# Second slabs' low parts on GpSimd or inside the norm, the last squares of a norm summed by TensorE, and the root ahead of the split

## The chip, the cores and the metric
The kernel runs on one core of a Trainium2 chip. The metric is device time in microseconds (us) of one execution. The profile is of one execution, taken by the hardware profiler; in it PE is TensorE's matmuls, PEld its weight loads, DVE is VectorE, ACT ScalarE, POOL GpSimd, SP the queue of SyncE that issues most DMAs. L12 is line 12 of the kernel before.

## What is computed
Two transformer blocks and a hybrid block with a mixture of experts, for one sequence of 512 tokens and 1024 channels, all in float32. What bears on the change is that every layer begins with an RMS norm of the residual stream h, modulated by a scale and a shift, and then multiplies by a large weight matrix:

```python
def rms_norm(x, g):
    xf = x.astype(jnp.float32)
    y = xf * lax.rsqrt(jnp.mean(xf * xf, axis=-1, keepdims=True) + EPS)
    return (y * g.astype(jnp.float32)).astype(x.dtype)

sh, sc, gt = _ada(mod, 0)
h = h + 0.5 * gt * swiglu(modulate(rms_norm(h, norm_g[l, 0]), sh, sc), ffn_w_in[l, 0], ffn_w_out[l, 0])
u = modulate(rms_norm(h, norm_g[l, 1]), sh, sc)
y = dilated_mixer(u, ...)          # layer 0;  nsa_mixer(u, ...) in layer 1
h = h + gt * y
h = h + 0.5 * gt * swiglu(modulate(rms_norm(h, norm_g[l, 2]), sh, sc), ffn_w_in[l, 1], ffn_w_out[l, 1])
# behind layer 0: shared_kv of the normed h; behind layer 1: hybrid_mixer, then peer_ffn
```

## The kernel before
**Data.** h lies in SBUF as eight tiles of 128 channels x 512 tokens (KT = 8). The normed and modulated x is kept as a high part xh (rounded to the matmul's format) and a low part xl (the rest). All weights come from one array of 331 slabs, 128 x 2048 float32 (1 MB) each, in the order in which they are used. A slab goes through three steps, in two alternating slots: load_slab (SP, into raw, waits on raw_free), split_hi (ScalarE rounds it into whi, waits on the load and on slab_used, TensorE's count of slabs it is done with) and split_lo (VectorE writes wlo = raw - whi and counts raw_free up). Three matmuls a product (hi x hi, hi x lo, lo x hi) follow when slab_ready (raw_free) says so.

**Stages.** They run one after another, each a block of its own with a program for every engine, and a barrier of all engines between two blocks: init, ffn00, the dilated attention (qkv projection, attention, twice, then the projection awo), ffn01, shared_kv (wkv), ffn10, the nsa attention (projection wq, attention, projection bwo), ffn11, the mixer (win, branches, wout), and peer. f is the number of a stage's first slab. The first slab's parts for a stage are made in the stage before it. Before the change so are the second slab's in all but qkv and ffn00. Where a norm's tail ends the stage, the high part is made by ScalarE ahead of the root (L495 in the ffn stages, L1039 in stage_out_projection) and the low part by VectorE behind the reciprocal (L540, L1083); shared_kv makes ffn10's at its end, which stays as it is.

**The tail of a norm.** As TensorE finishes the output tiles of an ffn's second matrix or of a projection, VectorE adds each into h (L533, L1071 or L1073), ScalarE squares it (norm_square, L299) into a ring of two tiles, and VectorE adds the squares one by one into `total` (norm_add, L308). TensorE's norm_total, when its last product is out, runs seven products that nobody reads (L314), sums `total` over its 128 channels by four matmuls against ones (L323; the profile counts two passes each), runs three more unread products, and spreads the result: ScalarE takes the root of it (norm_std, L346), VectorE the reciprocal (norm_rinv, L359), and TensorE's norm_spread (L366) copies it to all 128 partitions of a PSUM bank. Three unread products end the block.

**The head.** The next block begins with norm_start on TensorE (five unread products), and norm_low on VectorE with norm_high on ScalarE: for each of the eight tiles VectorE writes the scaled tile, h x gain x root, from SBUF and PSUM into a ring of two (L392), ScalarE adds the shift and rounds it into xh (L374), and VectorE writes xl = scaled + shift - xh (L398), whose two tiles lie in SBUF. One scaled tile is made ahead. TensorE takes the first slab tile by tile behind them (L413 to L417; L427 to L431 in qkv and wq, where its first slab has tiles 0 to 3 and the second slab tiles 4 to 7). `between` is a hook that norm_high calls behind tile 2 and norm_low behind tile 4; ffn00 makes its second slab there. In qkv of the first half the second slab is split after all eight tiles.

## Time and profile before

| | us, if nothing else is said |
|---|---|
| device time, median of 3 (lowest, highest) | 4014.19 (4013.3, 4015.83) |
| span of the profiled execution, first to last instruction | 4013.5 |
| TensorE busy | 3869.2 (96%) |
| VectorE busy | 2602.8 (65%) |
| ScalarE busy | 1598.1 (40%) |
| GpSimd busy | 556.3 (14%) |
| mean granted TensorE clock (1 is 2.4 GHz, 0.5 is 1.2 GHz) | 0.985 |

The profile gives no other time of that execution than its span. The norm boundaries are at these times of the span (the reciprocal, L359): 408.7 between ffn00 and qkv, 1009.4 between awo and ffn01, 1379.7 between ffn01 and wkv, 1811.7 between ffn10 and wq, 2112.6 between bwo and ffn11, 2481.5 between ffn11 and win, 2719.7 between wout and peer. A row of a timeline gives the start, the duration, the engine, the line, the operation with what it writes and reads, how many were merged (x3), and in brackets how long the engine was idle before it and what ended that. Starts of matmuls follow each other by 0.227 us at the full clock while each lasts 0.39, since they overlap.

### The profile page before, as it was taken

The numbers are of one execution on the slowest core, as the hardware profiler recorded it, in microseconds if no ns is written. First come the engines' busy times: TensorE is split into PE (matmuls) and PEld (weight loads), VectorE is DVE, ScalarE is ACT, GpSimd is POOL, SyncE is SP. The second block draws the span as 40 slices with busy tenths as digits, with TensorE's granted clock in tenths as the row PEclk, the third lists the DMA queues.
The fourth block names the chain that finished last, engine by engine and source line by source line (L and its number), as shares of the span: only waits on it lengthen the run. The fifth ranks groups of instructions, "written<-read, shape, count | busy, mean of one in ns | idle before, by whom it ended". The sixth has DMA issues, their size and how long they took to land. (4 is left out here: it accounts for less than half of the span.)

```text
span 4013.5 us, 54684 instructions
## 1 busy us (share of the span) xinstructions
PE 3869.2 (96%) x19575; PEld 3241.7 (81%) x19575; DVE 2602.8 (65%) x4763; ACT 1598.1 (40%) x2237; POOL 556.3 (14%) x565
## 2 busy tenths in 40 slices
PE   7999999999999989998999999999999999999998
PEld 6888786887888878886668887668889999988886
DVE  6642776766663466427854324768998888687887
ACT  3222335335322232225863222543346666533333
POOL 1100000000110011000000000000015555233332
PEclk9999999999999989998999999989999999999999
DMA  7632321322662256323012222113349999899997
GB/s 285 228 130 94 135 98 45 112 89 79 221 224 95 109 178 226 131 89 93 1 64 95 94 100 89 64 42 117 118 170 342 350 351 348 308 353 353 352 357 271
DMA packets 140839, 702.11 MB, mean 175 GB/s; under 512 B 18791, under 2 KB 20166, under 8 KB 95182
## 3 DMA queue, kind: packets, MB, share of 16 engines
q1 hardware_dynamic: 66734, 424.29, 29.2%
q0 software_dynamic: 73952, 275.81, 19.1%
q8 instruction: 92, 1.51, 0.2%
q14 instruction: 61, 0.50, 0.0%
HBM read 637.06 MB, written 59.80 MB: 174 GB/s over the span
## 5 line engine op out<-in xcount | busy, mean ns | idle before, releaser
L112 DVE TENSOR_TENSOR w_lo<-raw,w_hi 128x2048 fp32r<-128x2048 f32 x331 | 758.5, 2292 | 700.1 <-ACT w_hi L104 697.9
L124 PE MATMUL ps<-x_hi,w_hi 128*128 128x512 f32 (+1 forms) x2768 | 1032.3, 373 | 20.4 <-DVE w_lo L112 16.0
L125 PE MATMUL ps<-x_lo,w_hi 128*128 128x512 f32 (+1 forms) x2768 | 1022.7, 369 | 0.0
L126 PE MATMUL ps<-x_hi,w_lo 128*128 128x512 f32 (+1 forms) x2768 | 1022.2, 369 | 0.0
L104 ACT ACTIVATE w_hi<-raw 128x2048 fp32r<-128x2048 f32 x331 | 632.5, 1911 | 650.0 <-PE ps L126 421.4
L124 PEld LDWEIGHTS ps<-x_hi,w_hi 128*128 128x128 f32 x2768 | 521.0, 188 | 94.6 <-issue 17.4
L125 PEld LDWEIGHTS ps<-x_lo,w_hi 128*128 128x128 f32 x2768 | 521.1, 188 | 68.3
L126 PEld LDWEIGHTS ps<-x_hi,w_lo 128*128 128x128 f32 x2768 | 520.7, 188 | 67.7
L2483 POOL DMA_INDIRECT ph_rows<-in_peer_u,ph_names x88 | 156.8, 1782 | 1201.5 <-DVE ph_names L2855 981.5
L2566 PE MATMUL ps<-w_hi,px_gh 128*128 128x512 f32 x768 | 299.0, 389 | 2.0 <-issue 1.6
L2566 PE MATMUL ps<-w_lo,px_gh 128*128 128x512 f32 x768 | 298.8, 389 | 0.0
L2566 PE MATMUL ps<-w_hi,px_gl 128*128 128x512 f32 x768 | 298.8, 389 | 0.0
L480 ACT ACTIVATE silu<-ps 128x512 f32<-128x512 f32 x88 | 52.6, 598 | 560.1 <-PE ps L126 559.0
L124 PE MATMUL ps<-hid_hi,w_hi 128*128 (+1 forms) x704 | 273.9, 389 | 0.0
L126 PE MATMUL ps<-hid_hi,w_lo 128*128 (+1 forms) x704 | 273.9, 389 | 0.0
L125 PE MATMUL ps<-hid_lo,w_hi 128*128 (+1 forms) x704 | 273.9, 389 | 0.0
L133 PE MATMUL ps<-w_hi,x_hi 128*128 128x512 f32 (+1 forms) x672 | 257.2, 383 | 7.1 <-DVE w_lo L112 4.8
L134 PE MATMUL ps<-w_lo,x_hi 128*128 128x512 f32 (+1 forms) x672 | 255.7, 380 | 0.0
L135 PE MATMUL ps<-w_hi,x_lo 128*128 128x512 f32 (+1 forms) x672 | 255.6, 380 | 0.0
L510 DVE TENSOR_TENSOR silu<-silu,ps 128x512 f32<-128x512 f32 x88 | 60.4, 687 | 285.9 <-ACT silu L480 285.9
L184 DVE SCALAR_TENSOR_TENSOR ada_ring<-ada_ring,ps 128x1024 f32<-128x1024 f32 x160 | 187.7, 1215 | 19.6 <-DMA ada_ring<-in_w_ada 13.5
L2566 PEld LDWEIGHTS ps<-w_hi,px_gh 128*128 128x128 f32 x768 | 144.2, 188 | 32.6 <-issue 1.9
(432 smaller groups left out, 5661.6 us busy)
## 6 DMA issues: line engine op xcount, KB each, us to landing
raw<-in_slabs SPq DMA_DIRECT2D x331, 1024.0 KB, 4.9
ada_ring<-in_w_ada POOLq DMA_DIRECT2D x160, 512.0 KB, 5.6
act_dram<-px_act SPq DMA_DIRECT2D x64, 384.0 KB, 6.6
gate_dram<-ps_g SPq DMA_DIRECT2D x12, 2048.0 KB, 11.6
px_g<-gate_dram POOLq DMA_DIRECT2D x32, 768.0 KB, 8.1
px_ai<-act_dram POOLq DMA_DIRECT2D x64, 384.0 KB, 6.5
h_dram<-h SPq DMA_DIRECT2D x2, 2048.0 KB
h<-h_dram SPq DMA_DIRECT2D x2, 2048.0 KB, 8.2
```

Source lines behind the costliest of these rows:

```text
L104: k.nc.scalar.activation(k.whi[:, c % 2, :], k.raw[:, c % 2, :], ACT.Copy).then_inc(k.hi_in, 1)
L112: nc.vector.tensor_tensor(k.wlo[:, c % 2, :], k.raw[:, c % 2, :], k.whi[:, c % 2, :].bitcast(F32), ALU.subtract).then_inc(k.raw_free, 1)
L124: mm(out, hi, rhs_hi, start=start, stop=False)
L125: mm(out, hi, rhs_lo, start=False, stop=False)
L126: return mm(out, lo, rhs_hi, start=False, stop=stop)
L133: mm(out, x_hi, hi, start=start, stop=False)
L134: mm(out, x_hi, lo, start=False, stop=False)
L135: return mm(out, x_lo, hi, start=False, stop=stop)
L184: ve.scalar_tensor_tensor(slot, slot, 1.0, self.c, ALU.mult, ALU.mult, accum_out=k.mod[:, bass.ds(16 * i + m + 8 * self.base, 1)]).then_in ...
L510: nc.vector.tensor_tensor(sil[:, c % 2, :], sil[:, c % 2, :], bank(k, 2 + c % 2), ALU.mult).then_inc(prod_ready, 1)
L2483: gp.indirect_dma_start(row_of(n), None, d["peer_u" if n < P else "peer_v"], bass.IndirectOffsetOnAxis(names[:, n % P:n % P + 1], 0)).then ...
L2566: last = nc.tensor.matmul(bank(k, 2 * r + dh), x, w[:, slot, at:at + T], start=first and half == 0 and n == 0, stop=final and half == 1 an ...
```

## The change
It has four parts.

1. **Low parts on GpSimd.** ffn01, ffn11, shared_kv, the mixer's first stage and peer get a GpSimd program (or a first step in it) that makes the second slab's low part, second_lo. It is gone from VectorE at the end of the stage before. VectorE waits for it behind norm_low (second_lo_done).
2. **Low parts inside the norm.** In wq the second slab's low part is made by VectorE behind tile 4 of norm_low; in qkv of the first half so too, and its high part by ScalarE behind tile 2 of norm_high. For that the first of three rounds in qkv's programs for ScalarE and VectorE is written out ahead of the loop.
3. **Sums by TensorE.** VectorE adds the squares of six of the eight tiles; those of the last two are summed over channels by TensorE directly from the ring, before and after `total`. The three unread products behind norm_spread go.
4. **The root ahead of the split.** ScalarE takes the root (norm_std) before it makes the high part of the second slab.

```diff
+def second_lo(k, gp, f):
+    gp.wait_ge(k.hi_in, f + 2)
+    k.nc.gpsimd.tensor_tensor(k.wlo[:, (f + 1) % 2, :], k.raw[:, (f + 1) % 2, :], k.whi[:, (f + 1) % 2, :].bitcast(F32),
+                              ALU.subtract).then_inc(k.raw_free, 1)
+
+
+def second_lo_done(k, ve, f):
+    ve.wait_ge(k.raw_free, f + 4)
...
+BY_ADDS = KT - 3
+
+
+def norm_total(k, pe, total, ring, rb=SUM_BANK):
     x, w = k.xh[:, 0, 0:P], k.xl[:, 0, :]
     pe.wait_ge(k.n["h"], KT * k.norms + 2)
     unread_products(k, 0, x, w, 7)
-    pe.wait_ge(k.n["summed"], KT * k.norms + KT - 1)
-    for b in range(NB):
-        last = k.nc.tensor.matmul(bank(k, SUM_BANK, 1, b), total[:, b * P:(b + 1) * P], k.ones[:, 0:1],
-                                  start=b == 0, stop=b == NB - 1)
-    last.then_inc(k.n["summed"], 1)
+
+    def sums(squares, first=False, final=False):
+        for b in range(NB):
+            last = k.nc.tensor.matmul(bank(k, SUM_BANK, 1, b), squares[:, b * P:(b + 1) * P], k.ones[:, 0:1],
+                                      start=first and b == 0, stop=final and b == NB - 1)
+        return last
+    pe.wait_ge(k.n["sq"], KT * k.norms + KT - 1)
+    sums(ring[:, (KT - 2) % 2, :], first=True)
+    pe.wait_ge(k.n["summed"], KT * k.norms + BY_ADDS)
+    sums(total)
+    pe.wait_ge(k.n["sq"], KT * k.norms + KT)
+    sums(ring[:, (KT - 1) % 2, :], final=True).then_inc(k.n["summed"], KT - BY_ADDS)
     unread_products(k, 0, x, w, 3)
     norm_spread(k, pe, rb, k.norms + 1)
-    unread_products(k, 0, x, w, 3)
...
+        by_gpsimd = name in ("ffn01", "ffn11")
...
             if ada:
                 ada.load_c(gp, d)
+            if by_gpsimd:
+                second_lo(k, gp, f)
...
+            norm_std(k, act)
             if f > 0:
                 split_hi(k, 0, f + n_in + n_out + 1)
-            norm_std(k, act)
...
-                if n > 1:
+                if 1 < n <= BY_ADDS + 1:
                     norm_add(k, ve, n - 1, sil, total)
-            norm_add(k, ve, KT - 1, sil, total)
             norm_rinv(k, ve)
-            if f > 0:
-                split_lo(k, 0, f + n_in + n_out + 1)
...
+            if hf == 0:
+                norm_high(k, act, rot, norm[1], lambda: split_hi(k, 0, f + 1))
+                group(0, True)
+                with act.Fori(0, 2) as g:
+                    group(g + 1)
...
+            if hf == 0:
+                norm_low(k, ve, rot, norm[0], norm[1], SUM_BANK, permuted=True, between=lambda: split_lo(k, 0, f + 1))
...
             for m in range(KT - 2, KT):
                 norm_square(k, act, m, m, ring, total)
+            norm_std(k, act)
             split_hi(k, 0, f + 5)
-            norm_std(k, act)
...
-            norm_add(k, ve, KT - 2, ring, total)
-            norm_add(k, ve, KT - 1, ring, total)
             norm_rinv(k, ve)
-            split_lo(k, 0, f + 5)
...
-            norm_low(k, ve, q[:, 0], norm[0], norm[1], SUM_BANK)
+            norm_low(k, ve, q[:, 0], norm[0], norm[1], SUM_BANK, between=lambda: split_lo(k, 0, f + 1))
...
             norm_low(k, ve, ct, mod[0], mod[1], SUM_BANK)
+            second_lo_done(k, ve, f)
```

TensorE between bwo's last product and ffn11's head, before (L314 unread products, L323 the sum against ones, L366 the spread; L979 and L542 are the end of one block and the start of the next):

```order
5923 L314 MATMUL ps<-x_lo,x_hi 128x512 [waits norm_h]
5924 L314 MATMUL ps<-x_lo,x_hi 128x512 x6
5925 L323 MATMUL ps<-ones,norm_ring 128x1 [waits norm_summed]
5926 L323 MATMUL ps<-ones,norm_ring 128x1 x3
5927 L314 MATMUL ps<-x_lo,x_hi 128x512 x3
5928 L366 MATMUL ps<-ident,norm_r 128x128 [waits norm_r4]
5929 L366 MATMUL ps<-ident,norm_r 128x128 x3
5930 L314 MATMUL ps<-x_lo,x_hi 128x512 x3
5931 L979 UNCONDITIONAL_BRANCH
5932 L542 UNCONDITIONAL_BRANCH [waits barrier_Pool_Activation_PE_DVE_SP_release]
```

The same place of the same engine after (line numbers are the changed kernel's: L324 unread products, L337 sums, L385 the spread):

```order
5935 L324 MATMUL ps<-x_lo,x_hi 128x512 [waits norm_h]
5936 L324 MATMUL ps<-x_lo,x_hi 128x512 x6
5937 L337 MATMUL ps<-ones,norm_ring 128x1 [waits norm_sq]
5938 L337 MATMUL ps<-ones,norm_ring 128x1 x3
5939 L337 MATMUL ps<-ones,norm_ring 128x1 [waits norm_summed]
5940 L337 MATMUL ps<-ones,norm_ring 128x1 x3
5941 L337 MATMUL ps<-ones,norm_ring 128x1 [waits norm_sq]
5942 L337 MATMUL ps<-ones,norm_ring 128x1 x3
5943 L324 MATMUL ps<-x_lo,x_hi 128x512 x3
5944 L385 MATMUL ps<-ident,norm_r 128x128 [waits norm_r4]
5945 L385 MATMUL ps<-ident,norm_r 128x128 x3
5946 L1019 UNCONDITIONAL_BRANCH
```

One sum has become three, each with a wait of its own, and nothing stands between the spread and the end of the block. The other six tails of this form read alike.

ScalarE at the same place, before (L104 is split_hi, L299 the squares, L346 the root):

```order
894 L104 ACTIVATE w_hi<-raw 128x2048 [waits slab_used,raw_in0]
895 L299 ACTIVATE norm_ring<-h 128x512 [waits norm_summed,norm_h] x4
896 L104 ACTIVATE w_hi<-raw 128x2048 [waits slab_used,raw_in1]
897 L346 ACTIVATE norm_r<-ps,eps 128x4 [waits norm_summed]
898 L979 UNCONDITIONAL_BRANCH
```

ScalarE there after (L309 the squares, L365 the root):

```order
919 L104 ACTIVATE w_hi<-raw 128x2048 [waits slab_used,raw_in0]
920 L309 ACTIVATE norm_ring<-h 128x512 [waits norm_summed,norm_h] x4
921 L365 ACTIVATE norm_r<-ps,eps 128x4 [waits norm_summed]
922 L104 ACTIVATE w_hi<-raw 128x2048 [waits slab_used,raw_in1]
923 L1019 UNCONDITIONAL_BRANCH
```

The second slab's high part is now the last instruction of ScalarE's block.

GpSimd from the end of the nsa attention to the first gather of peer, after (L118 is second_lo; L71 clears semaphores between blocks):

```order
222 L71 ISA x5
223 L488 UNCONDITIONAL_BRANCH
224 L118 TENSOR_TENSOR w_lo<-raw,w_hi 128x2048 [waits hi_in]
225 L462 UNCONDITIONAL_BRANCH
226 L71 ISA [waits barrier_Pool_Activation_PE_DVE_SP_gather]
227 L71 ISA x4
228 L1970 UNCONDITIONAL_BRANCH
229 L118 TENSOR_TENSOR w_lo<-raw,w_hi 128x2048 [waits hi_in]
230 L1965 UNCONDITIONAL_BRANCH
```

Before, GpSimd had no instruction in these blocks but the clearing of semaphores; now a 128x2048 subtraction is the first of ffn11's and of the mixer's.

## Rows read from the trace of the kernel before

**Rows 1.** Page, first part: busy us, share of the span, instructions of each engine.
```profile
PE 3869.2 (96%) x19575; PEld 3241.7 (81%) x19575; DVE 2602.8 (65%) x4763; ACT 1598.1 (40%) x2237; POOL 556.3 (14%) x565
```

**Rows 2.** Timeline (start, us, engine, line, operation), TensorE, tail of bwo.
```profile
2108.79 1.75 PE L314 MATMUL ps<-x_lo,x_hi 128*128 128x512 f32 x7
2111.19 1.05 PE L323 MATMUL ps<-ones,norm_ring 128*128 128x1 f32 x8 [0.65 <-DVE norm_ring L308]
2112.10 0.94 PE L314 MATMUL ps<-x_lo,x_hi 128*128 128x512 f32 x3
2112.88 1.08 PE L366 MATMUL ps<-ident,norm_r 128*128 128x128 f32 x8
2113.72 0.94 PE L314 MATMUL ps<-x_lo,x_hi 128*128 128x512 f32 x3
2115.32 1.40 PE L314 MATMUL ps<-w_hi 128*128 128x512 f32 x5 [0.66 <-PEq L979]
```

**Rows 3.** Timeline, ScalarE and VectorE, the same tail of bwo.
```profile
2110.31 1.89 ACT L104 ACTIVATE w_hi<-raw 128x2048 fp32r<-128x2048 f32 x1
2112.28 0.26 ACT L346 ACTIVATE norm_r<-ps,eps 128x4 f32<-128x4 f32 x1
...
2112.67 2.26 DVE L112 TENSOR_TENSOR w_lo<-raw,w_hi 128x2048 fp32r<-128x2048 f32 x1
```

**Rows 4.** Timeline, TensorE and VectorE, tail of ffn01.
```profile
1374.90 1.75 PE L314 MATMUL ps<-x_lo,x_hi 128*128 128x512 f32 x7
...
1379.24 0.94 PE L314 MATMUL ps<-x_lo,x_hi 128*128 128x512 f32 x3
...
1379.81 2.26 DVE L112 TENSOR_TENSOR w_lo<-raw,w_hi 128x2048 fp32r<-128x2048 f32 x1
```

**Rows 5.** Timeline, TensorE, tail of ffn10, at the half clock.
```profile
1812.61 1.91 PE L366 MATMUL ps<-ident,norm_r 128*128 128x128 f32 x8
1814.17 1.19 PE L314 MATMUL ps<-x_lo,x_hi 128*128 128x512 f32 x3
```

**Rows 6.** Timeline of qkv's head, and one stretch: its us, busy of five engines, clock.
```profile
422.18 0.73 DVE L398 SCALAR_TENSOR_TENSOR x_lo<-dp_rot,mod,x_hi 128x512 fp32r<-128x512 f32 x1
...
423.99 0.74 DVE L398 SCALAR_TENSOR_TENSOR x_lo<-dp_rot,mod,x_hi 128x512 fp32r<-128x512 f32 x1
...
430.82 0.80 PE L133 MATMUL ps<-w_hi,x_hi 128*128 128x512 f32 x1 [4.78 <-DVE w_lo L112]
...
435.95 0.39 PE L133 MATMUL ps<-w_hi,x_hi 128*128 128x512 f32 x1
...
430.80:434.00 3.20, 3.18 (x8) 2.51 (x9) 2.90 (x4) 0.00 (x0) 0.00 (x0) 0.50 0.58 195
```

**Rows 7.** Timeline, GpSimd and VectorE in nsa; one line of the source view (ns min/median/max).
```profile
1986.73 1.04 POOL L1557 CAST nsa_q<-nsa_qT 64x1024 fp32r<-64x1024 f32 x1 [5.16 <-PE ps L1570]
...
1986.70 0.69 DVE L1730 CUSTOM_DVE_ANT_0 na_sm<-ps,nsa_causal 128x512 f32<-128x512 f32 x1
...
1987.44 0.35 DVE L1736 SCALAR_TENSOR_TENSOR na_ng<-na_mx,nsa_rs 128x4 f32<-128x4 f32 x1
...
1901.62 0.17 DVE L1736 SCALAR_TENSOR_TENSOR na_ng<-na_mx,nsa_rs 128x4 f32<-128x4 f32 x1
...
L1730 DVE CUSTOM_DVE_ANT_0 na_sm<-ps,nsa_causal x128: 280/486/692, 1881.6 to 2049.3; 128x128 f32<-128x128 f32 x32, 128x256 f32<-128x256 f32 x32, 128x384 f32<-128x384 f32 x32, 128x512 f32<-128x512 f32 x32
```

**Rows 8.** Timeline, VectorE and GpSimd, head of wq; GpSimd's first in ffn01.
```profile
1815.79 1.41 DVE L392 SCALAR_TENSOR_TENSOR nq_q<-h,gain,ps 128x512 f32<-128x512 f32 x2 [1.71 <-PEq L443]
1817.32 0.75 DVE L398 SCALAR_TENSOR_TENSOR x_lo<-nq_q,mod,x_hi 128x512 fp32r<-128x512 f32 x1
...
1818.77 0.75 DVE L398 SCALAR_TENSOR_TENSOR x_lo<-nq_q,mod,x_hi 128x512 fp32r<-128x512 f32 x1
...
1816.33 0.14 POOL L1342 MEMSET nq_kcp<- 64x64 f32 x1 [185.66 <-POOLq L443]
...
1014.30 0.57 POOL L163 DMA_DIRECT2D ada_ring<-in_c_rows  x1 [240.69 <-issue]
```

More of the change, by code:

```diff
@@ L465, in _ @@
             two_step(sp, n_in + n_out, lambda i, c: load_slab(k, sp, i, c), f + 2)
-        if ada:
-            @blk.gpsimd
-            def _(gp):
+        by_gpsimd = name in ("ffn01", "ffn11")
+        @blk.gpsimd
+        def _(gp):
+            if ada:
                 ada.load_c(gp, d)
+            if by_gpsimd:
+                second_lo(k, gp, f)
+            if ada:
                 with gp.Fori(0, 3) as i:
@@ L709, in _, with group @@
             act.sem_inc(s["trc"], 4)
-            if hf == 0:
-                norm_high(k, act, rot, norm[1])
-            with act.Fori(0, 3) as g:
+            def group(g, first=False):
                 for c in range(3):
-                    split_hi(k, 3 * g, f + 2 * c + 1)
+                    if not (first and c == 0):
+                        split_hi(k, 3 * g, f + 2 * c + 1)
                     if c > 0:
@@ L726, in _ @@
                         nc.scalar.activation(ss[:], ss[:], ACT.Sqrt).then_inc(s["std"], 1)
+            if hf == 0:
[3 more added lines that the diff above has]
+                    group(g + 1)
+            else:
+                with act.Fori(0, 3) as g:
+                    group(g)
         @blk.vector
@@ L731, in _, with group @@
             ve.sem_inc(s["freed"], 4)
-            if hf == 0:
-                norm_low(k, ve, rot, norm[0], norm[1], SUM_BANK, permuted=True)
-            ve.wait_ge(s["const"], 32)
-            with ve.Fori(0, 3) as g:
+            def group(g, first=False):
                 for c in range(3):
-                    split_lo(k, 3 * g, f + 2 * c + 1)
+                    if not (first and c == 0):
+                        split_lo(k, 3 * g, f + 2 * c + 1)
                     if c == 2:
@@ L778, in _ @@
                             ve.wait_ge(s["rot"], n)
+            if hf == 0:
+                norm_low(k, ve, rot, norm[0], norm[1], SUM_BANK, permuted=True, between=lambda: split_lo(k, 0, f + 1))
+            ve.wait_ge(s["const"], 32)
+            if hf == 0:
+                group(0, True)
+                with ve.Fori(0, 2) as g:
+                    group(g + 1)
+            else:
+                with ve.Fori(0, 3) as g:
+                    group(g)
     k.heads += hf == 0
@@ L1129, in stage_shared_kv, with _ @@
         k2 = k.ps[0:NC, 7 * T:7 * T + 2 * HD].rearrange("p (h d) -> p h d", h=2)
+        @blk.gpsimd
+        def _(gp):
+            second_lo(k, gp, f)
         @blk.sync
@@ L1230, in _ @@
             norm_low(k, ve, ct, mod[0], mod[1], SUM_BANK)
+            second_lo_done(k, ve, f)
             ve.wait_ge(s["const"], 80)
@@ L1926, in stage_mixer_in, with _ @@
         blk = ctx.enter_context(nc.Block(no_gpsimd_drain=True))
+        @blk.gpsimd
+        def _(gp):
+            second_lo(k, gp, f)
         @blk.sync
@@ L1980, in _ @@
             norm_low(k, ve, sig, norm[0], norm[1], SUM_BANK)
+            second_lo_done(k, ve, f)
             split_lo(k, 0, f + 2)
@@ L2485, in gather @@
                     asked[0] = n + 1
+            second_lo(k, gp, f)
             gp.wait_ge(s["names"], HEADS)
@@ L2913, in _ @@
             norm_low(k, ve, norm_ring, norm[0], norm[1], 5)
+            second_lo_done(k, ve, f)
             ve.wait_ge(s["const"], 48)
```

6 lines of the change are left out of this document (3 added, 3 removed).

## The prediction
> **What bounds the kernel now.** First the page's busy shares: TensorE works for 96% of the span [rows 1], so time can only be won or lost where it waits or runs slow. What the change touches is seven norm boundaries, each of them a tail (the end of one block, where the squares are summed and the root is taken) and a head (norm_low and norm_high of the next block), so I read the timelines of those stretches next, engine by engine. In a tail after a projection TensorE ends its last product, runs seven unread products, waits 0.65 us for VectorE's last add, sums the squares, and 0.78 us later spreads the root [rows 2]. The reader is to see which engine arrives last at the end of the block: VectorE's low part of the second slab ends at 2112.67 + 2.26 = 2114.93 and TensorE's last three unread products at 2114.66, and the next block starts at 2115.32 [rows 2, 3]. At the half clock (ffn10) it is TensorE that is last: 1814.17 + 1.19 = 1815.36 [rows 5]. In a head VectorE sets the pace and TensorE follows tile by tile.
>
> **The tails.** The change removes two adds and adds eight matmuls against ones. A sum over four blocks occupies TensorE for 2112.10 - 2111.19 = 0.91 us [rows 2], so three sums are 2.74 us, one after the other, and they can't start before the seven unread products have issued, 7 x 0.227 = 1.59 us after those began (six steps and a last product of 0.39 make the 1.75 of the row).
> - Behind an ffn: 1374.90 + 1.59 + 2.74 = 1379.23, and today TensorE is through its sum at 1379.24 [rows 4]. The adds saved are worth nothing there: TensorE takes as long to sum as VectorE took to add. The root comes at the same time as before.
> - Behind a projection: 2108.79 + 1.59 + 2.74 = 2113.12, today 2112.10: the root comes 1.0 us **later**. VectorE had only two adds behind the last tile, TensorE now has three sums behind its unread products.
>
> Then the split: ScalarE's high part (1.89 us) stands ahead of the root now and ends 0.08 us before it starts [rows 3]; it costs nothing where it is. Put behind the root it ends last. Behind ffn01 and ffn11: root over at 1379.24 + 0.13 + 0.04 + 0.26 = 1379.7, split over at 1381.6, where today VectorE's low part ends at 1379.81 + 2.26 = 1382.07 [rows 4]: 0.5 us won, twice. Behind bwo and wout: root over at 2113.12 + 0.43 = 2113.55, split over at 2115.4 against 2114.93: 0.5 lost, twice. Behind ffn00 and ffn10 (half clock) the three unread products behind the spread go, and it ends at 1812.61 + 1.91 = 1814.52 against 1815.36 [rows 5]: 0.8 won, twice. Awo lies between the last two kinds; I take 0.2 won. Sum of the tails: -1.0 + 1.0 - 1.6 - 0.2 = **-1.8 us**. If the half clock went from the tails, ScalarE's split would be the gate in them too, and 1 us each more is won in three; that is the far end, -4.8.
>
> **The second slab of qkv.** TensorE has multiplied tiles 0 to 3 with the first slab and then stands idle for 4.78 us, because the second slab's low part is made behind all of norm_low; it then starts at the half clock (0.50 granted), and its first chain of twelve products takes until 435.95 [rows 6]. Now the high part goes behind ScalarE's third tile and the low part behind VectorE's fifth. The high part (1.89 us) fits: one tile of x_hi is all that ScalarE has to make in each 1.81 us of VectorE's, and the next one's scaled tile isn't there earlier. VectorE: low of tile 4 ends at 422.18 + 0.73 = 422.9, low of the slab at 425.2, then 1.81 us a tile [the step from 422.18 to 423.99, rows 6]: tiles 5, 6, 7 are through at 427.0, 428.9, 429.7. TensorE reaches the second slab at 426.04, waits 1 us or so at two tiles, and has its first chain done at 430.4 instead of 435.95: **-5.5 us**, of which 2.4 come from the clock (twelve products took 5.13 us and not 2.72) and are lost again if it halves all the same: -3.1 to -5.5. In nsa the same insertion in norm_low costs nothing: there TensorE needs 12 x 0.227 = 2.72 us a tile in the first part and VectorE 1.45 [1817.32 to 1818.77, rows 8], and four tiles of that slack, 5.1 us, cover the 2.26.
>
> **GpSimd's low parts, the costly term.** In ffn01, wkv, ffn11, win and peer the low part (128x2048, two inputs) now starts on GpSimd with the block, while VectorE begins norm_low. How the two share SBUF the trace shows where GpSimd casts 64x1024 in nsa: a tiny VectorE instruction with two inputs in SBUF that begins inside such a cast takes 0.35 us instead of 0.17 and ends within 0.02 us of the cast's end (1986.73 + 1.04 = 1987.77 and 1987.44 + 0.35 = 1987.79), while one of 512 elements with an input in PSUM, begun beside the cast, takes 0.69, and 0.692 is the longest of all 128 of that line [rows 7]. So VectorE's two-input instructions wait for the whole of GpSimd's, the others don't. Norm_low alternates: the scaled tile reads h and PSUM (free), the low part of x reads two tiles in SBUF (blocked), and VectorE keeps its order, so one blocked instruction stops them all.
> The duration isn't in the trace. Lower bound: a one-input cast of 1024 elements takes 1.04 us, so twice the elements 2.08. Upper: four times the elements read, 4 x 1.04 = 4.16. I take 4.16, since with the two-input form the cast's one stream of reads becomes two. GpSimd's first instruction comes 0.54 us behind VectorE's first, the first blocked one 1.53 us behind it [rows 8]. So x's first low part waits until 0.54 + 4.16 = 4.70 instead of 1.53: 3.2 us, and nothing makes it up, as VectorE paces all eight tiles. In ffn01 a DMA issue of 0.57 stands ahead [rows 8]: 3.7. Sum 4 x 3.2 + 3.7 = **+16.5 us**; with 2.08 it is 5 x 2.08 less, +6.1. What VectorE no longer does (2.26 us in each tail) was beside other work and is counted in the tails. second_lo_done finds it made: VectorE gets there eight tiles of 1.45 us later, 11.6 us against 4.7. Queued behind GpSimd's instruction are ffn01's ada loads, and on SP the load of slab f+3, which waits for that low part; both are some 4 us later and are read only when the head's eight tiles are through.
> The Trainium skill, "SBUF — State Buffer", section "SBUF: two separate sides", says the same of this pair: an exclusive lock, held for the full instruction, against GpSimd also for VectorE instructions with two SBUF inputs; the row of 0.35 us agrees. "GPSIMD Engine Reference", section 3.1, gives 4497 ns for this very shape, which no run here shows yet; by it the term would be 5 x 0.34 = 1.7 us more and the time 4027.9.
>
> **The clock in those heads.** TensorE is left idle there for about 3 us. After an idle stretch of 4.78 us the granted clock fell to 0.50 and cost 2.4 us [rows 6]; behind the shorter idle stretches of the tails it fell in ffn10 (spread 1.91 us) and not in bwo (1.08) [rows 2, 5]. I take half of that price in half of the five heads, 5 x 0.6 = **+3.0**, with 0 and 5 x 2.4 = 12 as ends.
>
> **Sum.** -1.8 - 5.5 + 16.5 + 3.0 = +12.2 us. The profiled execution's span is 4013.5; the median of the runs shown, 4014.19, lies 0.7 over it, within their spread (4013.3 to 4015.83), so I add to the median: 4026.4.
>
> **Rivals.**
> - *No blocking* (faster side): GpSimd's accesses slip between VectorE's, or its instruction is cut into pieces. Then the GpSimd term and the clock term are 0, and -1.8 - 5.5 gives 4006.9, down to 4003.9 without the half clock in the tails. For it: the cast in the trace is half as many partitions and never ran against a long two-input instruction that began after it. Against: the 0.35 row. It decides from about 1.5 us of blocking per head (7.3 / 5).
> - *GpSimd is quick*: 2.08 us. -7.3 + 6.1 + 1 = 4014, no change.
> - *The clock falls in every head* and stays down into the products: 12 instead of 3, 4035.4.
> - *A tail that isn't gated as I read it*: if the block's end doesn't wait for ScalarE's split, bwo and wout lose nothing and the tails give 1.5 more. It moves each of the above, and has no chance of its own.
>
> **Chances.** Forecast as worked out 0.60 (with the durations between 3 and 4.5 us: 4018 to 4031), clock in every head 0.10, quick GpSimd 0.13, no blocking 0.14, the rest 0.03. The range goes from the no-blocking case to the forecast's own upper end and somewhat into the clock case: 4007 to 4033. Within 0.2% is +-8 us (about what a measurement of this kernel tells from no change): over 4022.2 lie most of the forecast (0.52) and the clock case, 0.62 in all; within it the low end of the forecast, quick GpSimd and nearly half of no blocking, 0.28; below 4006.2 the rest, 0.10.
>
> **What would show it.** In the profile after: GpSimd rows of 4 to 4.5 us in five heads; behind them one x_lo instruction of VectorE drawn out to 3 to 4 us (or begun that much later), and all eight tiles later by as much; granted clock 0.5 in some of those heads; in the tails three sums of 0.91 us back to back with the root 1 us later behind bwo and wout, and ScalarE's w_hi as the last instruction of the block; in qkv no idle of 4.78 us. Wrong would be: x_lo at 0.75 us beside a running GpSimd instruction, which is the first rival; a GpSimd row of about 2 us, the second; a root that isn't later behind bwo, which would mean that sums against ones go faster than 0.91 us when they stand in a row.

## The result: 0.4% slower, and where the time went

The changed kernel takes 4032.07 us (median of 5 runs, 4028.03 to 4032.61) beside 4015.4 us for the kernel before (4013.3 to 4016.79), a ratio of 1.0039 with a 95% interval of 1.0028 to 1.0049: 16.7 us slower. The forecast was 4026.4 in a range of 4007 to 4033, with 0.62 for slower.

The profiled execution has a span of 4030.8 us where before has 4013.5, 17.3 more. First the page's busy line, which answers [rows 1]:

```profile
PE 3886.5 (96%) x19666; PEld 3259.7 (81%) x19666; DVE 2599.6 (64%) x4744; ACT 1597.5 (40%) x2237; POOL 583.2 (14%) x570
```

TensorE is busy for 17.3 us more and idle for as long as before. So the waits won and lost about cancel, and that part of the loss is in matmuls that are more (the sums) or slower (the clock). So the boundaries have to be read one by one.

**A head that GpSimd works in.** Timeline of the changed kernel, head of ffn01 (start, us, engine, line, operation, the idle time before it and who ended it); it answers [rows 8], whose x_lo took 0.75 us:

```profile
1007.47 1.41 DVE L411 SCALAR_TENSOR_TENSOR silu<-h,gain,ps 128x512 f32<-128x512 f32 x2 [2.24 <-PEq L1019]
...
1008.65 4.54 POOL L118 TENSOR_TENSOR w_lo<-raw,w_hi 128x2048 fp32r<-128x2048 f32 x1
1009.01 4.74 DVE L417 SCALAR_TENSOR_TENSOR x_lo<-silu,mod,x_hi 128x512 fp32r<-128x512 f32 x1
...
1013.81 1.22 PE L436 MATMUL ps<-x_lo,w_hi 128*128 128x512 f32 x2 [3.52 <-DVE x_lo L417]
...
1014.83 0.63 PE L432 MATMUL ps<-x_hi,w_hi 128*128 128x512 f32 x1
...
1014.45 0.75 DVE L417 SCALAR_TENSOR_TENSOR x_lo<-silu,mod,x_hi 128x512 fp32r<-128x512 f32 x1
```

The reader is to see four things. The first x_lo, ready at 1009.01, ends 0.56 us after GpSimd does (1008.65 + 4.54 = 1013.19). TensorE stands for 3.52 us at its first tile. The next x_lo is back at 0.75, so one instruction alone was held. And the product behind the wait lasts 0.63 us where it takes 0.39 at full clock. The source view of GpSimd's line gives its five instructions (ns, min/median/max), and the windows of three of the five heads the granted clock (the last but two of the columns; win and peer have 0.94 like ffn01 and ffn11):

```profile
L118 POOL TENSOR_TENSOR w_lo<-raw,w_hi x5: 4539/4553/4564, 1008.7 to 2733.9; 128x2048 fp32r<-128x2048 f32 x5
1007.50:1034.00 26.50, 22.41 (x92) 17.83 (x91) 22.14 (x25) 11.07 (x13) 8.77 (x9) 0.94 0.65 238
1380.70:1408.00 27.30, 24.43 (x145) 20.89 (x146) 24.10 (x33) 8.56 (x10) 4.55 (x1) 0.98 0.45 171
2120.00:2146.50 26.50, 23.53 (x95) 18.64 (x95) 18.01 (x19) 10.04 (x12) 4.55 (x1) 0.94 0.23 82
```

Before, all five stretches were granted 1.00; ffn01's for one:

```profile
1013.80:1040.30 26.50, 25.95 (x113) 20.60 (x112) 22.21 (x32) 11.59 (x14) 5.35 (x10) 1.00 0.72 269
```

Four of them are now at 0.94: 0.06 x 26.5 = 1.6 us each, which together with wkv's 0.5 makes 6.9. Wkv's part isn't the head's own: the clock had already fallen in the tail ahead of it, where the spread takes 1.85 us.

**A tail.** Timeline of the tail of bwo in the changed kernel, TensorE, ScalarE and VectorE; it answers [rows 2, 3]:

```profile
2111.72 1.75 PE L324 MATMUL ps<-x_lo,x_hi 128*128 128x512 f32 x7
...
2113.31 2.84 PE L337 MATMUL ps<-ones,norm_ring 128*128 128x1 f32 x24
...
2116.18 0.26 ACT L365 ACTIVATE norm_r<-ps,eps 128x4 f32<-128x4 f32 x1 [2.84 <-PE ps L337]
2116.34 1.90 ACT L104 ACTIVATE w_hi<-raw 128x2048 fp32r<-128x2048 f32 x1
...
2117.43 1.91 PE L385 MATMUL ps<-ident,norm_r 128*128 128x128 f32 x8
```

The three sums stand back to back (24 matmuls, 2.84 us), start 1.59 us behind the unread products' start, and the root comes 2116.18 - 2111.72 = 4.46 us into the tail instead of 2112.28 - 2108.79 = 3.49: 1.0 us later, as worked out. What wasn't foreseen is the spread: 1.91 us, half clock, in a tail that ran at full clock before (1.08).

**qkv's head.** Timeline, VectorE and TensorE, answering [rows 6]:

```profile
422.08 2.28 DVE L112 TENSOR_TENSOR w_lo<-raw,w_hi 128x2048 fp32r<-128x2048 f32 x1
...
425.98 0.39 PE L143 MATMUL ps<-w_hi,x_hi 128*128 128x512 f32 x1
...
429.60 0.39 PE L143 MATMUL ps<-w_hi,x_hi 128*128 128x512 f32 x1
```

The idle 4.78 us is gone. The second slab starts at 425.98 and the last product of its first chain of twelve starts at 429.60 (before at 435.95). Against the block's first VectorE instruction (411.97, before 412.85) that is 17.6 us instead of 23.1: 5.5 us won.

**All boundaries in one table.** Each tail is measured from the start of the unread products behind the last true product to norm_low's first instruction in the next block; each head from there to the end of the last x_lo. All from the timelines, in us:

| | ffn00 | awo | ffn01 | ffn10 | bwo | ffn11 | wout | sum |
|---|---|---|---|---|---|---|---|---|
| tail, before | 8.97 | 8.52 | 7.56 | 8.88 | 6.72 | 7.69 | 6.57 | 54.9 |
| tail, changed | 7.60 | 7.08 | 7.26 | 6.78 | 8.24 | 6.92 | 6.87 | 50.8 |
| head behind it | qkv | ffn01 | wkv | nsa | ffn11 | win | peer | five with GpSimd |
| head, before | 14.58 | 11.84 | 11.85 | 11.84 | 11.85 | 11.18 | 11.23 | 58.0 |
| head, changed | 16.77 | 15.84 | 15.24 | 13.93 | 14.85 | 14.38 | 14.50 | 74.8 |

Tails -4.2, qkv -5.5, the five heads +16.9: +7.2 us. The span grew by 17.3. Of the other 10, 6.9 are slower matmuls in the heads' windows. The last 3 us lie outside both, and only in part can it be read where. Peer is 15.7 us late at its second kind of product (2767.88 - 2752.18) and 17.3 at its end, and in between the changed kernel was granted 0.83 in 2985:2995 and in 3488:3498, where before has 1.00 in 2960:3000 and 3460:3500. In the dilated attention it was granted 0.83 in 680:690 (before 1.00 in 660:700), and 1.5 us of qkv's 5.5 are lost again there. The GpSimd part alone, below, is granted 1.00 in both places of peer, so these stretches aren't shown to come from the change; each trace is of one execution.

### The profile page after: what moved, and what is told of

It reads as the page before. It is cut to its first block and busy times, and to the rows that moved or that the text cites. A ratio compares the mean times of both kernels' runs of the same rounds, so it can differ in the third digit from the quotient of the medians.

```text
span 4030.8 us, 54766 instructions
## 1 busy us (share of the span) xinstructions
PE 3886.5 (96%) x19666; PEld 3259.7 (81%) x19666; DVE 2599.6 (64%) x4744; ACT 1597.5 (40%) x2237; POOL 583.2 (14%) x570
## 5 line engine op out<-in xcount | busy, mean ns | idle before, releaser
L112 DVE TENSOR_TENSOR w_lo<-raw,w_hi 128x2048 fp32r<-128x2048 f32 x326 | 747.4, 2293 | 701.0 <-ACT w_hi L104 699.0
L104 ACT ACTIVATE w_hi<-raw 128x2048 fp32r<-128x2048 f32 x331 | 632.6, 1911 | 651.5 <-PE ps L136 421.6
```

The lines of the kernel that those rows point to most:

```text
L104: k.nc.scalar.activation(k.whi[:, c % 2, :], k.raw[:, c % 2, :], ACT.Copy).then_inc(k.hi_in, 1)
L112: nc.vector.tensor_tensor(k.wlo[:, c % 2, :], k.raw[:, c % 2, :], k.whi[:, c % 2, :].bitcast(F32), ALU.subtract).then_inc(k.raw_free, 1)
```

## Experiments: the four parts apart

### The GpSimd part alone

```diff
 (kernel before, ffn01, wkv, ffn11, win, peer)
+ gpsimd: second_lo(k, gp, f)            # at the block's start
+ vector: second_lo_done(k, ve, f)       # behind norm_low
- vector: split_lo(k, 0, f + 5)          # in the tail ahead, likewise behind ffn01 and ffn11
```

> The kernel before with one part of the change alone: the low part of the second slab of ffn01, wkv, ffn11, win and peer is made by GpSimd at the block's start instead of by VectorE in the tail ahead. Sums, root, split and qkv stay as before. Theory (GpSimd holds SBUF for its whole 4.55 us, VectorE's first low part of x waits for its end, and TensorE, left idle, then runs some products at half clock): the five heads grow as in the changed kernel's trace, by 4.00, 3.39, 3.00, 3.20 and 3.27, together 16.9 us, the granted clock in four of them is 0.94 over 26.5 us, 1.6 us each or 6.4, and the tails win 0.3 each at most since TensorE's last unread products end there 0.3 before VectorE's low part did: 4014 + 16.9 + 6.4 - 1.5 = 4036. Rival A (the half clock comes from the changed tails, not from the wait in the head): 4029.5. Rival B (most of the changed kernel's loss is in its tails): below 4022.

Measured: 4035.48 us, before beside it 4015.24, ratio 1.0051 (1.0037 to 1.0064). The part alone costs 20.2 us, more than the whole change. Heads 15.85, 15.22, 14.85, 14.37, 14.49 (74.8 again); x_lo in ffn11's head:

```profile
2125.28 3.75 DVE L408 SCALAR_TENSOR_TENSOR x_lo<-silu,mod,x_hi 128x512 fp32r<-128x512 f32 x1
...
2129.73 0.74 DVE L408 SCALAR_TENSOR_TENSOR x_lo<-silu,mod,x_hi 128x512 fp32r<-128x512 f32 x1
```

The theory gave 4036. Rival B, that most of the loss was in the tails, has fallen: these tails are no longer than before (52.4 us together against 54.9). So has rival A, that the half clock came from the changed tails: behind these tails the five heads' windows are granted 0.87, 0.94, 0.94, 0.94 and 1.00. It isn't always the same four: here wkv falls and peer doesn't, in the changed kernel's trace it was the other way round.

### The qkv part alone

```diff
 (kernel before, stage_project_dilated as in the changed kernel)
- norm_high(k, act, rot, norm[1])
+ norm_high(k, act, rot, norm[1], lambda: split_hi(k, 0, f + 1))
- norm_low(k, ve, rot, norm[0], norm[1], SUM_BANK, permuted=True)
+ norm_low(k, ve, rot, norm[0], norm[1], SUM_BANK, permuted=True, between=lambda: split_lo(k, 0, f + 1))
```

> The kernel before with the qkv part alone: the second slab's high part goes behind ScalarE's third tile and its low part behind VectorE's fifth, with the loops' first pass written out. Theory: TensorE's idle 4.78 us and the half clock behind it go, -5.5 us: 4008.7. Rival (the clock halves there all the same, and only the wait goes): -3.1, 4011.1. If the loops written out cost instruction fetches: nothing gained, 4014.

Measured: 4009.28 against 4015.24, ratio 0.9986 (0.9977 to 0.9995): 6.0 us won, 5.5 expected. In the window 422 to 436 the granted clock is 1.00 where before has 0.76, and TensorE is busy for 12.94 us instead of 9.22.

### The sums alone

```diff
 (kernel before)
- pe.wait_ge(summed, KT - 1); four matmuls on total
+ four on square KT-2; four on total; four on square KT-1
- norm_add(k, ve, KT - 2, ...); norm_add(k, ve, KT - 1, ...)
```

> The kernel before with the three sums alone: the squares of the last two tiles are summed by TensorE and VectorE's adds for them go; the split stays ahead of the root, the low part stays in the tail, the last three unread products stay. Theory (the term of the prediction): nothing behind an ffn, the root 1.0 us later behind each of the three projections: 4015 + 3 = 4018, if the clock of the tails stays. Rival (the sums change where the half clock falls, 1 us and more a tail, either way): the tails that ran at half clock before (ffn00, awo, ffn10) may run at full clock, 4012 to 4015, or others fall, 4021.

Measured: 4015.52 against 4015.25, ratio 1.0000 (0.9991 to 1.0009). The root does come later behind the projections (the sums end 4.34 us into bwo's tail instead of 3.45, in wout 4.32 instead of 3.39), but the tails' sum grows by 1.4 only, 56.4: awo 9.00, bwo 8.92 and wout 7.48 are longer, ffn00 is 7.27 instead of 8.97 since it now runs at full clock (its spread takes 1.08 us, before 1.91). The theory's 1.0 us is there in wout, the one tail behind a projection that stays at full clock: 0.9 us longer. The rival is there too: what moves with the clock in ffn00 (-1.7) and bwo (+2.2, of which the later sums are 0.9) is as large. The time can't choose between them, since its interval (3.6 us either way) holds the theory's +3 as well as nothing. In bwo the full-clock spread of 1.08 us became this:

```profile
2110.99 2.76 PE L327 MATMUL ps<-ones,norm_ring 128*128 128x1 f32 x24
...
2115.05 1.91 PE L376 MATMUL ps<-ident,norm_r 128*128 128x128 f32 x8
```

### The low parts back on VectorE, the root still ahead of the split

```diff
 (changed kernel)
- gpsimd: second_lo; vector: second_lo_done      # five heads
- nsa: between=lambda: split_lo(k, 0, f + 1)
+ norm_rinv(k, ve); split_lo(...)                # in six tails
```

> The changed kernel with the low parts of six second slabs (nsa's too) made by VectorE in the tail behind the reciprocal, as the kernel before makes them, but with the root still ahead of the split. Theory: the heads are as before (16.9 us of blocking and 6.4 of half clock gone), but the low part now waits for the split that stands behind the root, so the block ends 2.3 us later in six tails: 4032 - 23.3 + 6 x 2.3 = 4022.5. Rival (TensorE, idle for some 3 us behind the spread, falls to half clock at six heads' start): 1.6 us each more, 4032.

Measured: 4024.81 against 4015.25, ratio 1.0024 (1.0014 to 1.0035); 4022.5 was expected. The heads are those of before (11.85, 11.85, 11.84, 11.85, 11.18, 11.23). The six tails go to 9.15 to 9.50 us, since the low part waits for a split that stands behind the root; wout's tail:

```profile
2724.63 1.90 ACT L104 ACTIVATE w_hi<-raw 128x2048 fp32r<-128x2048 f32 x1
...
2726.56 2.29 DVE L112 TENSOR_TENSOR w_lo<-raw,w_hi 128x2048 fp32r<-128x2048 f32 x1 [1.62 <-ACT w_hi L104]
...
2729.55 1.54 PE L324 MATMUL ps<-w_hi 128*128 128x512 f32 x3 [3.39 <-DVEq L1017]
```

So the root ahead of the split is a loss as long as a low part that waits for that split stands in the tail. The converse isn't so: the fastest versions below have the low part on GpSimd and the split ahead of the root.

The rival was right about the clock and wrong about its price. TensorE stands idle behind the spread for 3.1 to 3.4 us in the four of these tails that run at full clock (ffn01 and ffn10, at half clock already, have 1.6 and 2.5), and in the first 10 us of all six heads the granted clock is 0.83 to 0.85, where before has 1.00. But the time is 2.3 us over the theory and not 9.6. Why it costs so little here, and more in the heads that GpSimd blocks, is open.

## Experiments: what holds VectorE, and what halves the clock

### The held instruction reads PSUM

```diff
 (changed kernel, five heads)
- norm_high(k, act, sil, ...);  norm_low(k, ve, sil, ...)
+ norm_high(k, act, InPsum(k, (1, 3)), ...);  norm_low(k, ve, InPsum(k, (1, 3)), ...)
+ class InPsum: tile t of the ring is bank(k, banks[t % 2])   # win (5, 6); wkv, peer (0, 1)
```

> The changed kernel, with the scaled tiles of the five heads written to two free PSUM banks instead of SBUF, so that VectorE's low part of x reads one operand from PSUM and one from SBUF, and GpSimd's low part stays where it is. Theory (GpSimd's instruction holds off only VectorE instructions with two inputs in SBUF): x_lo takes about 0.7 us beside the running GpSimd instruction, the 16.9 us of blocking and 6.4 us of half clock go: 4032 - 23.3 = 4008.7, plus whatever the PSUM tiles cost in time per tile (0.1 us x 40 would be 4). Rival (GpSimd holds off every VectorE instruction, or every one that touches SBUF, for its length): 4032 as it is, with a row of 4 us on the scaled tile or x_lo.

Measured: 4008.08 against 4015.24, ratio 0.9981 (0.9972 to 0.9990). 24 us less than the changed kernel, 23.3 expected, and faster than before. Head of ffn11, VectorE and GpSimd:

```profile
2108.15 1.41 DVE L411 SCALAR_TENSOR_TENSOR ps<-h,gain,ps 128x512 f32<-128x512 f32 x2 [2.14 <-PEq L1027]
2108.34 4.61 POOL L118 TENSOR_TENSOR w_lo<-raw,w_hi 128x2048 fp32r<-128x2048 f32 x1 [107.14 <-POOLq L1027]
...
2109.66 0.75 DVE L417 SCALAR_TENSOR_TENSOR x_lo<-ps,mod,x_hi 128x512 fp32r<-128x512 f32 x1
...
2111.11 0.75 DVE L417 SCALAR_TENSOR_TENSOR x_lo<-ps,mod,x_hi 128x512 fp32r<-128x512 f32 x1
```

Both x_lo of 0.75 us run inside one GpSimd instruction of 4.61 us. The heads take 11.78, 11.79, 11.78, 11.11, 11.16: nothing is left of the blocking, and the PSUM tiles cost no time. The instruction does the same arithmetic on the same shape; only where one operand lies has changed. That is what "two inputs in SBUF" predicts, and it excludes that GpSimd's instruction holds off VectorE as such. The Trainium skill, "SBUF — State Buffer", section "SBUF: two separate sides", has the rule in this form (an exclusive lock for the whole instruction, taken against GpSimd by a VectorE instruction with two SBUF inputs); the traces agree in both halves, 3.75 to 4.74 us with two inputs in SBUF and 0.75 with one.

### TensorE kept busy in the wait

```diff
 (changed kernel, mm3_tile, five heads)
+    if t == 0: unread_products(k, bank, whi, whi, 11)
     norm_tile(k, pe, t)
```

> The changed kernel, with eleven unread products (128x512) put between x_hi's products and the wait for x_lo at the first tile of the five heads whose low part GpSimd makes, so that TensorE is busy for 11 x 0.227 = 2.5 us of the 2.5 to 3.5 us in which it waited. Theory (the idle time brings the half clock): granted clock 1.00 in these heads instead of 0.94, 6.4 us less, 4032 - 6.4 = 4025.6; VectorE's rows stay as they are (x_lo of 3.75 to 4.74 us). Rival (the half clock doesn't come from this idle time): 4032, with 0.94 as before. If unread products delay the true ones: up to 4034.

Measured: 4023.65 against 4015.24, ratio 1.0022 (1.0013 to 1.0031). The eleven products give 8.4 us back, and the heads are as long as in the changed kernel (15.89, 15.30, 14.89, 14.43, 14.56). Head of ffn01 on VectorE and TensorE, and its window:

```profile
1008.54 4.80 DVE L417 SCALAR_TENSOR_TENSOR x_lo<-silu,mod,x_hi 128x512 fp32r<-128x512 f32 x1
...
1009.65 2.65 PE L324 MATMUL ps<-w_hi 128*128 128x512 f32 x11
...
1013.96 0.40 PE L432 MATMUL ps<-x_hi,w_hi 128*128 128x512 f32 x1
...
1007.00:1033.50 26.50, 24.84 (x106) 19.09 (x105) 22.12 (x25) 11.00 (x13) 8.84 (x9) 1.00 0.66 238
```

Products behind the wait take 0.40 us and the granted clock is 1.00 in all five. So the half clock of the heads is a consequence of TensorE's idle 2.5 to 3.5 us. Its price is 8.4 us between the medians (6.4 were expected, and 6.9 stand in the windows of one execution), beside 16.9 for the wait itself.

### GpSimd's instruction in four pieces

```diff
 (changed kernel, second_lo)
- k.nc.gpsimd.tensor_tensor(wlo[:, slot, :], raw, whi, subtract)
+ for c in range(0, SLAB, SLAB // 4): k.nc.gpsimd.tensor_tensor(wlo[:, slot, c:c + SLAB // 4], ...)
```

> The changed kernel with GpSimd's low part cut into four instructions of 128x512. Theory (VectorE's instruction waits for the GpSimd instruction that is running, and for that one alone): four rows of about 4.55 / 4 = 1.14 us, the first x_lo waits for the end of one piece, is at most 1.14 + 0.75 = 1.9 us long, and then the two engines take turns; a head grows by 1 to 2 us and not by 3.0 to 4.0, TensorE's longest wait is 1.5 us and not 2.5 to 3.5, and the half clock of the heads goes: 4032 - 5 x 1.9 - 6.4 = 4016, with a growth of 1.5. Rival (GpSimd keeps SBUF over instructions that stand back to back): x_lo of 3.7 to 4.7 us again, 4032.

Measured: 4018.46 against 4015.25, ratio 1.0008 (0.9999 to 1.0017), so it isn't told apart from the kernel before; 4016 was expected. Growth of the five heads over before: 4.43, 0.87, 1.50, 0.93, 1.23. Four behave as expected; peer's head (VectorE), its GpSimd, then ffn01's:

```profile
2725.33 0.98 DVE L420 SCALAR_TENSOR_TENSOR x_lo<-px_act,x_hi 128x512 fp32r<-128x512 f32 x1
...
2727.01 1.01 DVE L420 SCALAR_TENSOR_TENSOR x_lo<-px_act,x_hi 128x512 fp32r<-128x512 f32 x1
...
2724.46 6.40 POOL L120 TENSOR_TENSOR w_lo<-raw,w_hi 128x512 fp32r<-128x512 f32 x4 [231.71 <-POOLq L1022]
...
1008.64 5.17 DVE L420 SCALAR_TENSOR_TENSOR x_lo<-silu,mod,x_hi 128x512 fp32r<-128x512 f32 x1
...
1008.30 4.95 POOL L120 TENSOR_TENSOR w_lo<-raw,w_hi 128x512 fp32r<-128x512 f32 x4
```

In peer the engines take turns: x_lo of 1.0 us instead of 0.68, and GpSimd's pieces 1.7 us instead of 1.3. In ffn01 one x_lo waited through all four pieces, 5.17 us. The theory as I had put it (the running instruction alone) is therefore right in four heads and wrong in one; what makes ffn01 different (its x_lo asks 0.34 us into the first piece, in peer 0.87) is open.

## Experiments: a version that beats both

The tails were left as the place where time is still to be had: in the kernel before, a tail behind a projection takes 6.6 or 6.7 us at full clock and 8.5 when the clock falls, one behind an ffn 7.6 or 7.7 and 8.9 or 9.0.

### Both halves of the split in the tail's idle time

```diff
 (changed kernel without GpSimd's part, six tails)
+ scalar: split_hi(...)     # ahead of the last square
+ vector: split_lo(...)     # ahead of the reciprocal
```

> A version meant to beat both: the changed kernel with the six second slabs split in the tail where both engines are idle, the high part by ScalarE ahead of its last square (as soon as TensorE is through the last product) and the low part by VectorE ahead of the reciprocal, while TensorE runs unread products and sums; GpSimd makes none. Theory: in wout's tail the split runs 2726.9 to 2728.8, the last square is done at 2729.4 and wanted by the third sum at 2730.1, the low part ends at 2731.1 and the root at 2731.2, so all is hidden; heads as before (-16.9 - 6.4) and the block no longer waits for the split (-0.5 in six tails): 4032 - 23.3 - 3 = 4005.7. Rival (the last square comes too late and the sums and the root with it, by 1 us in six tails): 4011.7. Rival (the tails fall to half clock, 1.1 us each, in up to six): 4012.

Measured: 4010.37 against 4015.25, ratio 0.9985 (0.9976 to 0.9994). Where the clock holds (wout, 6.58 us) all is hidden as worked out:

```profile
2711.51 1.92 ACT L104 ACTIVATE w_hi<-raw 128x2048 fp32r<-128x2048 f32 x1 [3.48 <-PE ps L136]
2712.84 2.73 PE L337 MATMUL ps<-ones,norm_ring 128*128 128x1 f32 x24
...
2713.46 2.29 DVE L112 TENSOR_TENSOR w_lo<-raw,w_hi 128x2048 fp32r<-128x2048 f32 x1 [1.31 <-ACT w_hi L104]
...
2715.61 0.26 ACT L365 ACTIVATE norm_r<-ps,eps 128x4 f32<-128x4 f32 x1 [1.67 <-PE ps L337]
```

But five of seven tails fall to half clock (8.61, 7.78, 8.94, 7.95, 9.23; the seven together 55.7), the second rival. The first is there in small: in the three tails behind an ffn that have this split, TensorE waits 0.32 or 0.33 us for the last square.

### Unread products between the sums

```diff
- unread_products(k, 0, x, w, 7); sums(...); sums(...); sums(...)
+ unread 3; sums(...); unread 2; sums(...); unread 2; sums(...)      # early split
+ unread 1; sums(...); unread 2; sums(...); unread 2; sums(...)      # PSUM tiles, split_hi ahead of the last square
```

> The version with the early split, with the same instructions of TensorE in the tail in another order: three unread products, first sum, two unread products, second sum, two unread products, third sum, instead of seven unread products and then three sums. Theory (the half clock that five of its seven tails show follows the 2.7 us in which TensorE runs sums of one column alone): these tails go back from 7.8 to 9.2 us to the 6.6 that two of them have at full clock; the seven took 55.7 us and would take 46.2: 4010.4 - 9.5 = 4001. Rival (the order of unread products and sums has nothing to do with the clock): 4010. If the products between the sums only delay them: a little over 4010.

> The version with the scaled tiles in PSUM and the low parts on GpSimd, with the high part of the second slab ahead of ScalarE's last square and five unread products instead of seven, one ahead of the first sum and two ahead of each of the others. Theory: VectorE has nothing to do in the tail but the reciprocal, so the root can come 2 x 0.227 = 0.45 us earlier than with seven, and no tail falls to half clock: seven tails of 6.6 - 0.45 = 6.15, together 43, instead of the 52.5 of the version with PSUM tiles: 4008.1 - 9.5 = 3998.6. Rival (the fewer unread products let the clock fall, 1.1 us a tail and more): 4007. Rival (one unread product ahead of the first sum is too few to cover the square it waits for, so TensorE waits instead): 4001.

Measured: 4013.67, ratio 0.9995 (0.9986 to 1.0004), and 4020.15, ratio 1.0010 (1.0001 to 1.0019), against 4015.11. Both theories fell: the tails grew to 58.8 and 62.8 us. Behind a projection the order costs nothing at full clock, and five products do give 0.45 us (wout 6.62 and 6.16); behind an ffn TensorE now waits for the first square (0.59 and 1.04 us below). The clock was expected to hold. In the first version (10.34, 6.82, 9.56, 7.36, 8.03, 10.02, 6.62) four tails fall instead of five: ffn00 falls now, and awo and ffn10, which fell with the early split, run at full clock. In the second (10.44, 8.22, 10.97, 9.60, 7.49, 9.88, 6.16) six fall, where the version with PSUM tiles and seven products has four. Ffn10's spread in the first version (early split: 1.91 us):

```profile
1810.41 1.07 PE L387 MATMUL ps<-ident,norm_r 128*128 128x128 f32 x8
```

The tail of ffn01 in the three versions: last of TensorE at full pace, first at half pace (early split, early split mixed, PSUM mixed):

```profile
1367.04 1.75 PE L324 MATMUL ps<-x_lo,x_hi 128*128 128x512 f32 x7
...
1372.69 1.70 PE L385 MATMUL ps<-ident,norm_r 128*128 128x128 f32 x8
```
```profile
1369.24 0.84 PE L324 MATMUL ps<-x_lo,x_hi 128*128 128x512 f32 x3
1370.67 1.05 PE L337 MATMUL ps<-ones,silu 128*128 128x1 f32 x8 [0.59 <-ACT silu L309]
...
1373.50 1.68 PE L337 MATMUL ps<-ones,silu 128*128 128x1 f32 x8
```
```profile
1370.56 0.39 PE L324 MATMUL ps<-x_lo,x_hi 128*128 128x512 f32 x1
1371.99 1.05 PE L337 MATMUL ps<-ones,silu 128*128 128x1 f32 x8 [1.04 <-ACT silu L309]
...
1373.63 1.70 PE L337 MATMUL ps<-ones,ada_ring 128*128 128x1 f32 x8
```

A set of eight took 0.95 us and then 1.70. With seven products straight behind the true ones the fall comes 5.7 us after the last true product, with three 4.3, with one 3.1. That would say that unread products are worth most straight behind the true ones, but the tail of ffn11 doesn't bear it out. There the tails begin at 2471.67, 2475.54 and 2478.49, and the first rows that are drawn out (a set of sums, then twice two unread products, which take 0.70 us at full clock) begin 3.8, 3.7 and 3.7 us later:

```profile
2475.43 1.70 PE L337 MATMUL ps<-ones,silu 128*128 128x1 f32 x8 [0.32 <-ACT silu L309]
```
```profile
2479.24 1.04 PE L324 MATMUL ps<-x_lo,x_hi 128*128 128x512 f32 x2
```
```profile
2482.20 0.90 PE L324 MATMUL ps<-x_lo,x_hi 128*128 128x512 f32 x2
```

Fewer products in front also opened the waits for a square. So where the unread products are worth most isn't shown; what is shown is that spreading them between the sums doesn't keep the clock up in every tail.

### One sum, an unbroken block of products, PSUM tiles

```diff
 (version with PSUM tiles; tail of the kernel before)
- three sums;  root ahead of split
+ VectorE's adds and one sum;  split ahead of root;  no unread products behind the spread
+ unread_products(k, 0, x, w, 7)   # second version: 9
```

> A version meant to beat both: the version with the scaled tiles in PSUM and the low parts on GpSimd, with the tail of the kernel before (VectorE's adds, one sum behind seven unread products, the split ahead of the root) but without the three unread products behind the spread. Theory: the block's end waits for the spread alone, since no low part stands in the tail. Behind a projection the spread begins 4.03 us after the last product (2719.96 - 2715.93 in the trace of before), lasts 1.08 at full clock, and the block starts 0.5 later: 5.6 us; behind an ffn 5.12 + 1.08 + 0.5 = 6.7. Seven tails 3 x 5.6 + 4 x 6.7 = 43.6 instead of the 52.5 of the version with PSUM tiles: 4008.1 - 8.9 = 3999.2. Rival (three or four tails fall to half clock, as in the kernel before, 1.1 us each): 4003. Rival (all fall): 4007.

> The same with nine unread products instead of seven ahead of the one sum, so that TensorE stands idle 0.15 us behind a projection and 1.2 us behind an ffn, and not 0.6 and 1.7. Theory (the clock falls the later, the more TensorE works ahead of the sum): one or two tails fewer at half clock, 1 to 2 us less than with seven. Rival (the two products change nothing): the same time within 1 us. If they delay the sum: up to 1 us more behind the three projections.

Measured: 4003.93, ratio 0.9971 (0.9960 to 0.9982), and 4002.12, ratio 0.9968 (0.9956 to 0.9980), against 4015.22 beside them. Both beat the kernel before, and their medians are the lowest of all versions; against the version with PSUM tiles and three sums (4008.08, 0.9972 to 0.9990) the intervals still overlap a little. The tail changes in several ways at once here (one sum, split ahead of the root, nothing behind the spread), and what each gives isn't separated. The tails take 7.53, 6.29, 8.12, 7.65, 5.80, 6.78, 5.65 (47.8) with seven products and 6.75, 6.30, 7.33, 6.88, 5.80, 7.60, 5.65 (46.3) with nine. The 1.8 us between the two go the way that was expected, but their intervals overlap, so nine against seven isn't shown. Nor did fewer tails fall: three in each trace. The tail of wout with nine:

```profile
2701.98 2.20 PE L324 MATMUL ps<-x_lo,x_hi 128*128 128x512 f32 x9
...
2706.03 1.07 PE L375 MATMUL ps<-ident,norm_r 128*128 128x128 f32 x8
...
2707.63 1.41 DVE L401 SCALAR_TENSOR_TENSOR ps<-h,cols,ps 128x512 f32<-128x512 f32 x2 [1.74 <-PEq L1018]
```

## The prediction, step by step

- **GpSimd blocks x_lo once per head: right.** Five x_lo of 3.75 to 4.74 us, the next ones 0.75, all tiles later by as much. Forecast 16.5 us, measured 16.9. Inside this term three steps missed and nearly cancelled, which is luck: the duration was taken as 4.16 us (four times the cast of [rows 7]) and is 4.55, and GpSimd's start was taken 0.54 us behind VectorE's and is 0.20 in ffn11 and 0.28 in peer (2120.16 - 2119.96, 2733.87 - 2733.59); and a held x_lo ends 0.56 us behind GpSimd's instruction, where the working has it begin there and take its full 0.75. For the duration the 4497 ns of the Trainium skill, "GPSIMD Engine Reference", section 3.1, was nearer to the measured 4553; the sum by it is 4026.4 + 1.7 = 4028.1, not the 4027.9 that stands in the prediction.
- **The clock in those heads: right in kind, mis-sized.** The step "half of that price in half of the five heads" gave 3.0 us. Both halves were too small. Four heads were slowed and not 2.5, since the 2.5 to 3.5 us of idle time that the blocking leaves were enough nearly every time. And a fall cost 1.6 us by the windows (2.1 by the 8.4 us that filling the waits gave back), not 1.2. With 8.4 in place of 3.0 the sum is 4031.8, and the measured median is 4032.07. That they meet so closely is luck in part: the tails gave 2.4 us more than forecast, and 17.3 - 7.2 - 6.9 = 3.2 us of the span's growth lie where the prediction has no term.
- **The tails: -1.8 forecast, -4.2 in the trace.** The root is 1.0 us later behind bwo (4.46 against 3.49) as worked out, ScalarE's split ends last where the tail runs at full clock (not in bwo, where the spread ends at 2117.43 + 1.91 = 2119.34 and the split at 2118.24), and ffn11 and wout are at -0.8 and +0.3 against -0.5 and +0.5. What was missed is the clock again, both ways: awo and ffn10 lost their half clock (-1.4 and -2.1), bwo got one (+1.5 instead of +0.5). The tail at half clock was treated as a property of the place; it moves when the work in the tail is changed. In the run with the sums alone the root's delay of 0.9 us is in the trace, and the time, with 3.6 us either way, can't show it.
- **qkv: right.** -5.5 forecast, -5.5 between the traces, -6.0 alone.
- **nsa: right.** Its head grows from 11.84 to 13.93 us on VectorE, and TensorE stands idle in the 26 us from the block's start for 0.26 us before and 0.25 us now. From its head to its last product nsa is 2.3 us longer all the same, but 2.1 us longer also in the run with the sums alone, whose nsa head is that of before.
- **The rivals.** "No blocking" would have been 4006.9; the version with PSUM tiles, where the blocking really is gone, takes 4008.1, so that sum was sound and only its condition false. "The clock falls in every head" (4035.4) was the nearest other: four of five.

## To carry to other kernels

Before work goes to GpSimd beside VectorE, look at what VectorE reads meanwhile: an instruction with both inputs in SBUF waits for GpSimd's to end, and one with an input in PSUM doesn't, so moving a staging tile into a free PSUM bank turned a loss of 17 us into a gain of 7 here. Count for each wait of TensorE of some 3 us in such a place the half clock behind it, up to 1.6 us here, and fill the wait with products that nobody reads. Spread unread products between the other work of a short tail only with a measurement: here it made the tails longer.

## What the runs showed of the hardware

- GpSimd's two-input instruction of 128x2048 takes 4.55 us (median of five) in the changed kernel and with the GpSimd part alone, 4.61 where unread products fill TensorE's wait, and 4.63 with PSUM tiles. The first three hold VectorE off alike, so the difference isn't VectorE's work alone; its cause is open.
- Cut into four, the pieces take 1.27 us while VectorE waits and 1.73 where the engines take turns, and one head in five let all four pass before VectorE's instruction. Short pieces soften the blocking and don't do away with it.
- A two-input instruction of VectorE that waited for GpSimd's ends 0.56 us behind it (1013.75 and 1013.19 in ffn01), while alone it takes 0.75.
- The half clock followed TensorE's idle time at the start of a block in three arrangements: idle for 2.5 to 3.5 us behind GpSimd's blocking, four of five heads fell; idle for 3.1 to 3.4 us behind a late low part, all four whose tail had run at full clock; filled with eleven unread products, none of five.
